# State-space mixer of a hybrid layer: decay exponents by two 32-row products, and the scaling of a chunk placed behind the next chunk's masked decays

## What is computed

```python
acum = cumsum(dt * a)                                     # per head, over the chunk's 64 tokens
seg = acum[..., :, None] - acum[..., None, :]
decay = where(causal, exp(where(causal, seg, 0)), 0)
y_diag = einsum(cb[:, :, None] * decay, xdt)              # cb = cm . bm, xdt = x * dt
y_off = einsum(cm, s_prev) * exp(acum)[..., None]
y = (y_diag + y_off + x * d_skip) * silu(z)
y = rms_norm(y per group) * norm_g
```

## Time and profile before

| what | value |
|---|---|
| median of 3 runs | 1448.69 us (1448.61 to 1450.59) |
| span of the profiled execution | 1447.4 us |
| the profiled execution's own time | not listed apart; the median is 1.3 us above its span |
| PE busy | 1422.7 us, 98% of the span |
| DVE, ACT, POOL busy | 727.2, 411.7, 221.4 us |
| state-space stage, PE | 465.07 to 621.40 us, five chunks of 31.27 us |

### The profile page before, as it was taken

The page is one execution under the profiler, slowest core; times in us unless marked ns, Lnnn a source line. Parts: engine busy times, 40 slices in busy tenths (PEclk is TensorE's granted clock), DMA queues, the critical chain, the costliest instruction groups (busy, mean ns, idle before and its releaser), DMA issues.

```text
span 1447.4 us, 32378 instructions
## 1 busy us (share of the span) xinstructions
PE 1422.7 (98%) x13553; PEld 1031.3 (71%) x13553; DVE 727.2 (50%) x1360; ACT 411.7 (28%) x847; POOL 221.4 (15%) x183
## 2 busy tenths in 40 slices
PE   7999999999999999999999999999999999999997
PEld 6999777677776777777779985864466766757752
DVE  7443778887755677735467654623312112211217
ACT  2333444443422454333533211111111111111112
POOL 3784113130110000020003000011010000000000
PEclk9999999999999999999999999999999999999999
DMA  7897573754244544566568639699999999999996
GB/s 286 190 194 155 129 219 105 205 174 134 73 132 141 140 119 120 185 184 190 150 228 209 213 115 388 244 402 413 425 427 428 428 427 428 428 428 425 430 410 264
DMA packets 157907, 375.76 MB, mean 260 GB/s; under 512 B 102241, under 2 KB 110833, under 8 KB 139841
## 3 DMA queue, kind: packets, MB, share of 16 engines
q1 hardware_dynamic: 141936, 346.64, 67.7%
q0 software_dynamic: 7152, 16.85, 3.4%
q10 hardware_dynamic: 8672, 10.20, 2.1%
HBM read 329.24 MB, written 51.95 MB: 263 GB/s over the span
## 4 chain that ended last, share of the span: by engine, by line
PE 88%; DVE 6%; DMA 2%; DVEq 2%; ACT 1%; issue 1%; SPq 0%; ACTq 0%
PE PS L725 22%; PE PS L1296 15%; PE PS L1315 8%; PE PS L742 7%; PE PS L1142 6%; PE PS L1263 6%; PE PS L809 3%; DVE region L1823 2%; PE PS L1184 2%; PE PS L1268 2%; DVE region L1830 2%; PE PS L1206 1%; DMA region<-w_in 1%; PE PS L817 1%; PE PS L1122 1%
## 5 line engine op out<-in xcount | busy, mean ns | idle before, releaser
L725 PE MATMUL PS<-h0T,region 128*128 128x320 f32 x1360 | 390.3, 438 | 2.9 <-issue 1.6
L1428 ACT ACTIVATE region<-PS 128x320 f32<-128x320 f32 (+5 forms) x351 | 146.0, 427 | 664.8 <-PE PS L725 227.8
L725 PEld LDWEIGHTS PS<-h0T,region 128*128 128x128 f32 x1360 | 251.6, 190 | 110.8 <-issue 12.9
L1296 PE MATMUL PS<-region 128*64 128x512 f32 x1024 | 228.1, 592 | 0.0
L1296 PEld LDWEIGHTS PS<-region 128*64 128x64 f32 x1024 | 117.6, 137 | 101.6 <-issue 49.8
L1823 DVE TENSOR_TENSOR region<-region 128x512 f32<-128x512 f32 (+10 forms) x237 | 165.4, 717 | 35.9 <-DMA region<-wo 5.7
L1428 ACT ACTIVATE region<-region 128x256 f32<-128x256 f32 (+10 forms) x229 | 99.5, 465 | 100.3 <-DVEq L2243 24.5
L1315 PE MATMUL PS<-region,history 128*64 128x512 f32 x512 | 119.2, 597 | 1.1 <-ACTq L1763 0.5
L1823 DVE TENSOR_TENSOR history<-region,PS 128x256 f32<-128x256 f32 x32 | 13.5, 421 | 200.5 <-ACTq L1758 200.5
L1428 ACT ACT_TABLE_LOAD x77 | 98.8, 1283 | 25.5 <-ACTq L1475 9.5
L1830 DVE SCALAR_TENSOR_TENSOR region<-region,feature_vectors 128x320 f32<-128x320 f32 (+1 forms) x103 | 76.9, 747 | 54.1 <-ACTq L1504 41.0
(11 more groups left out here) (248 smaller groups left out, 1582.8 us busy)
## 6 DMA issues: line engine op xcount, KB each, us to landing
region<-moe_w SPq DMA_DIRECT2D x65, 2048.0 KB, 29.8
region<-moe_w SPq DMA_DIRECT2D x65, 1024.0 KB, 28.5
region<-w_in SPq DMA_DIRECT2D x115, 512.0 KB, 5.6
region<-wo SPq DMA_DIRECT2D x32, 512.0 KB, 4.4
expert_rows<-region SPq DMA_DIRECT2D x20, 512.0 KB, 7.0
region<-expert_rows SPq DMA_DIRECT2D x5, 2048.0 KB, 16.6
projected<-region ACTq DMA_DIRECT2D x59, 167.5 KB, 3.6
region<-projected SPq DMA_DIRECT2D x10, 768.0 KB, 6.6
```

Source lines behind the costliest of these rows:

```text
L725: last = mm(PS[:, 6 + i % 2, 0:NTOK], WR[:, i, k, :], H0T[:, k, :], start=(k == 0), stop=(k == KT - 1))
L1296: last = mm(PS[tiles(i), 2, :], XE[:, k, tiles(i)], W13[r][i][:, k * 512:k * 512 + 512], start=(k == 0), stop=(k == KT - 1))
L1428: return nc.scalar.activation(out, in_, f, **kw)
```

## The change

The constants and vectors on rows 32 to 63 are copied to rows 64 to 95 as well: three small loads on SP, of the bias and `a` in VEC, of LH, and of the second half of PM (pairs 8 to 15) in the place of the first. PM and RD are 8 wide instead of 16: on rows 32 to 63 RD holds pairs 0 to 7, on rows 64 to 95 pairs 8 to 15. The dt rows of a chunk come by two transfers, rows 0 to 63 as before and rows 32 to 63 once more into 64 to 95 (for chunk 0 a third one for rows 96 to 127), and the waits for `rows_in` count by 32. Each product of L990 takes 32 rows instead of 128, the two on different rows. The rest of the chunk's program stays but for `late(c - 1)`, which DVE now does after the SEG products (`ss_mt`) instead of before `step_in(c + 1)`.

```diff
-        LH, PM, SEL, TRI = (CON[:, a:a + n] for a, n in ((C_LH, 128), (C_PM, 16), (C_SEL, 32), (C_TRI, 128)))
+        LH, PM, SEL, TRI = (CON[:, a:a + n] for a, n in ((C_LH, 128), (C_PM, 8), (C_SEL, 32), (C_TRI, 128)))
...
-        RD, SEG, EBC, YO, YC, SN = take(16, L), take(16, L), take(16, L), take(16, L), take(16, L), take(2048)
+        RD, SEG, EBC, YO, YC, SN = take(8, L), take(16, L), take(16, L), take(16, L), take(16, L), take(2048)
...
+            sp.wait_ge(sem("vectors_in"), 32)
+            sp.dma_start(VEC[64:96, V_DTB:V_ALOG + 1], io['vecs'][32:64, V_DTB:V_ALOG + 1]).then_inc(sem("vectors_in"), 16)
+            sp.wait_ge(sem("consts_in_or_rows_kept"), 16)
+            sp.dma_start(CON[64:96, C_LH:C_LH + 128], io['consts'][32:64, C_LH:C_LH + 128]).then_inc(sem("vectors_in"), 16)
+            sp.dma_start(CON[64:96, C_PM:C_PM + 8], io['consts'][32:64, C_PM + 8:C_PM + 16]).then_inc(sem("vectors_in"), 16)
             sp.wait_ge(sem("zeroed_or_fetch_index"), 1)
...
             def dt_rows(c):
                 sp.wait_ge(sem("rows_free"), c + 1)
-                sp.dma_start(UM, ut[T_MISC, :, c, HIST:CW]).then_inc(sem("rows_in"), 16)
+                sp.dma_start(UM[0:64], ut[T_MISC, 0:64, c, HIST:CW]).then_inc(sem("rows_in"), 16)
+                sp.dma_start(UM[64:96], ut[T_MISC, 32:64, c, HIST:CW]).then_inc(sem("rows_in"), 16)
+                if c == 0:
+                    sp.dma_start(UM[96:128], ut[T_MISC, 96:128, c, HIST:CW]).then_inc(sem("rows_in"), 16)
...
                 for k in range(2):
-                    last = mm(bank(3 + k, 8, L), LH, RD[:, 8 * k:8 * k + 8, :], **full)
+                    rows = slice(32 + 32 * k, 64 + 32 * k)
+                    last = mm(bank(3 + k, 8, L), LH[rows], RD[rows], **full)
...
             def step_in(c):
-                dve.wait_ge(sem("rows_in"), c * 16 + 16)
+                dve.wait_ge(sem("rows_in"), c * 32 + 48)
...
-                tt(RD, over(AC, 16, 0, L), PM.unsqueeze(2).to_broadcast([128, 16, L]), mul)
+                tt(RD, over(AC, 8, 0, L), PM.unsqueeze(2).to_broadcast([128, 8, L]), mul)
...
                 tt(XDT, banks(0, 2, 16, L), DTS.unsqueeze(2).to_broadcast([128, 16, L]), mul)
-                if c > 0:
-                    late(c - 1)
                 if c is not NPC:
                     step_in(c + 1)
...
                 dve.drain().then_inc(sem("ss_mt"), 1)
+                if c > 0:
+                    late(c - 1)
                 tt(XET, XDT, ALS.unsqueeze(2).to_broadcast([128, 16, L]), mul)
```

More of the change, by code:

```diff
@@ L355, in gla_in @@
         def gla_in(c):
-            return ("conv_in" if c % 2 else "rows_in"), 16 * NCH + 32 * (c // 2 + 1)
+            return ("conv_in", 16 * NCH + 32 * (c // 2 + 1)) if c % 2 else ("rows_in", 32 * NCH + 16 + 32 * (c // 2 + 1))
         def rows_in_at(c):
@@ L1038, in _ @@
             pe.wait_ge(sem("phase_over"), ENG * 2)
+            pe.wait_ge(sem("vectors_in"), 80)
             for c in range(NCH):
@@ L1599, in _ @@
             meet(act, 2)
+            act.wait_ge(sem("vectors_in"), 80)
             a_(NA, VEC[:, V_ALOG:V_ALOG + 1], ACT.Exp)
@@ L2243, in ssm @@
                 dve.drain().then_inc(sem("variance"), 1)
+            dve.wait_ge(sem("vectors_in"), 80)
             step_in(0)
```

## The result

The changed kernel takes 1453.65 us (median of 11 runs, 1451.26 to 1456.59), the kernel before 1449.89 in the same comparison (11 runs, 1448.61 to 1452.49). The ratio is 1.0026, with a 95% interval of 1.0018 to 1.0034: 3.8 us slower, where 3.9 was forecast. The profiled execution itself took 1455.11 us at a span of 1453.2.

A forecast was written before the change was run, and what follows sets the result against it. PE bounds the kernel now, with the ring 0.43 us behind; moving late() makes the ring bound chunks 1 to 3. Waits 5.18 less 1.25 gained give +3.9 on 1448.69: 1452.6 us, range 1449.4 to 1455.4 for 8 in 10.

The forecast's parts named there:

- The ring: State-space mixer: DVE, ACT, SP's row loads, DVE again, one turn per chunk; 0.43 us from bounding, then 33.79, 32.59, 33.29.
- The sum: Five chunks: PE waits of 5.18 less 5 x 0.25 gained, +3.9 us on 1448.69, giving 1452.6 us; chance 0.60.
- PE would stay the bound: Rival: chunk 1's dt rows land within 5.98 us with nothing added, only the product's gain is left, 1447.4 us; chance 0.14.
- the second transfer lands 1.6 us behind the first: Rival, dt rows: the second transfer adds 1.6 us instead of 0.3 in three turns, 1456.5 us; chance 0.08.
- the pair runs one behind the other: Rival, two products of L990: they keep 1.80 us, plus 0.20 behind them, giving 1453.5 us; chance 0.08.
- the staircase: L990: second product starts with the first's second pass; 1.35 us instead of 1.80, less 0.20 behind, 0.25 net per chunk.
- The rival on full overlap: L990: both products run fully beside each other, 0.90 us instead of 1.35, giving 1451.7 us; chance 0.10.
- The waits before L1026: PE in chunks 1 to 3 waits for ss_yr from DVE: 1.32, 1.58 and 2.28 us.
- a wait for ss_mt instead of ss_yr: Sign of being wrong: PE waits before L1018, so ss_mt is late; the SEG products were forecast in time, at 511.6.
- The clock: PE in the five chunks: times were taken at a granted clock of 1.00, one chunk being 31.27 us.
- The second transfer: Dt rows of each chunk: their second part, issued behind the first on SP, adds 0.3 us per turn, between 0 and 0.6.
- The small loads at the RWKV stage: Three loads of VEC and CON on SP cost nothing: 1.95 us of cover for three issues of about 0.4.

The follow-up runs named there:

- The second trace: The changed kernel run once more, unedited, to see whether the clock drop in chunk 2 comes again: 1453.21 us, one run.

## Why the prediction was right, step by step

**The ring: right, shown.** The single terms measured what was put in. Root to conv issue: 504.66 - 499.67 = 4.99 (4.99 put in). Step_in to YO: 520.11 - 511.45 = 8.66 (8.60). YO to the next root: 532.59 - 520.11 = 12.48 (12.48). The turns, from reciprocal to reciprocal (497.85, 530.78, 564.79, 597.37), are 32.93, 34.01 and 32.58, 99.52 in all; the prediction had 33.79, 32.59 and 33.29, 99.67 in all. Each was off by about as much as its landing: from the first issue of the dt rows to step_in it took 6.37, 7.26 and 6.01 us where 7.3, 6.1 and 6.8 had been put in. From the first product of chunk 0 to that of chunk 4 took 128.81 us against 125.07 before, +3.74; the prediction had +4.15.

**The sum: near, in part by luck.** The single chunks were not met: 31.50, 35.45 and 31.15 us where 32.3, 32.6 and 33.3 had been forecast. Their sum is 98.10 against 98.2, since what the long landing and the drop of the clock added to chunk 2 came off chunk 3, and the misses of the landings largely cancelled. In the five chunks PE waited 4.40 us where 5.18 was forecast, and its own work fell by 0.67 (156.33 to 155.66) where 1.25 was forecast: the pair gave 2.75 in five chunks, the drop of the clock took 1.71 of it back, and 0.37 went into the first products behind the waits. That is +3.73 against +3.93. Without the drop PE's work would have been less and its waits longer, so the two misses are not independent; the mechanism stands on the experiments, not on this agreement.

**The rivals.** That PE would stay the bound needed 5.98 us or less in chunk 1; it was 6.37, a near miss. That the second transfer lands 1.6 us behind the first is not borne out: 0.5, 1.4 and 0.3. That the pair runs one behind the other is excluded by its 1.06 us.

**The pair: the gain was there, the staircase was not.** The step said "a staircase: the second product starts with the first's second pass", 1.35 us and 0.20 behind. The pair took 1.06 and the projection the 0.20 more: 0.55 net per chunk instead of 0.25. The start times show two records at 500.33 and two at 500.86, so both first passes run together, and then both second passes. Of the 1.06, 0.86 is two passes of 0.43, and 0.2 stands in front of them. Its cause is not shown, but the records fit a weight load that is less covered: the pair's first begins 0.07 us before the product ahead ends, where on 128 rows it begins 0.19 before. Of the 0.2, 0.1 is there on 128 rows as well (1.80 is four passes of 0.43 and 0.08; on one group of 32 rows it is 1.91). L1026's 1.93 reads the same way: the time of eight full-array records, 1.74, plus 0.2; I had taken the 0.2 for a staircase. The rival on full overlap was true in its mechanism, at 1.06 instead of its 0.90, and the Trainium skill (TensorE: Matmul & The Clock Gate, Part 3) had it right: matmuls in different row groups ran together; the trace agrees, 1.06 against 1.91 on one group. As the prediction said, this gain counts only where PE is the bound, so the total came out some 0.6 us lower than forecast by chunks 0 and 4, and by the turns of the ring not at all.

**The waits before L1026: right in kind.** Forecast 1.32, 1.58 and 2.28 us; measured 0.71, 2.00 and 0.35. In chunk 2 PE waited before L1027 too, 0.95, so ss_mt was late as well, after the longest way from issue to step_in, 7.26. The prediction had named a wait for ss_mt instead of ss_yr as a sign of being wrong; in this one chunk it came beside the wait for ss_yr.

**The clock: missed.** The prediction put a granted clock of 1.00 everywhere. The drop cost PE 1.71 us in chunk 2, but most of it was hidden: YO to root took 12.69 there (553.92 to 566.61) instead of 12.48, since DVE, not PE, set the turn. As an estimate, the 1.5 us that the ring did not lose came off PE's wait in chunk 3, which was 0.35 instead of the forecast 2.28.

**The carried state: missed.** PE waited 0.4 us in chunk 4. Its load follows the store of the old state, 7.55 us, and takes 6.30 more.

**The second transfer: sized at 0.3, none seen** when one transfer took the place of two. **The small loads at the RWKV stage: nothing shown.** The kernels with them start the state-space stage at 466.38 to 468.68, those without at 464.73 to 467.77, which overlap. In the first trace after, SP issues them from 143.12 to 144.51. PE is 1.15 us behind the trace of before once it has 200 records, 44.7 us into the span, and 1.14 behind once it has 1500, at 184.3, so no cost is seen there. In the profiled execution the stage began 3.7 us later than before; 1.15 of it came in the first 35 us, ahead of every edit, and the rest in small steps in the RWKV stage. The second trace began at 466.81. I take that as spread between executions; no run shows its cause. The 3.8 us of the medians are what the stage gives, from its first product to the next stage's first: 156.66 before, 160.32 and 160.59 in the two traces after.

## What to carry to other kernels

When PE is busy all the time, look for the ring of waits just behind it and read its slack, here 0.43 us: work moved out of the time that covers a transfer then costs its length less that slack in every turn, though no engine has more to do. Here 2.80 less 0.43 was to be expected, and with late() alone moved the three chunks grew by 1.25, 2.89 and 1.79 us, 1.98 in the mean. And look at the order in which a queue issues its loads: a small load that needs nothing should not stand behind one that waits for another engine; that alone turned a loss of 0.26% into a gain of 0.14%. A gain on PE inside such a ring should show only in the turns that PE still bounds; that is argued from the sums, and no run changes the pair alone.

## What the runs showed of the hardware that was not expected

- Two fp32 products of 512 columns on different groups of 32 rows take 1.06 us together, 1.80 on all rows one behind the other, 1.91 on one group of 32. Of the 1.06 some 0.2 is more than the two passes of 0.43, 0.1 of it more than the pair on all rows pays, and the full-array projection behind takes another 0.2 (4.50 instead of 4.31).
- The granted clock fell to half for 3.4 us behind a PE wait of 2.0 us, at the same place in both traces of the changed kernel, but not behind the same waits (0.8, then 2.0) in another kernel and not behind 2.5 us in a third. Twice in one trace (mean 0.75 over 6.2 us in chunk 2) it fell with no wait ahead of it, right behind two products on one group of 32 rows.
- A transfer of 32 KB and the same as two of 16 and 8 KB land equally late behind one of 768 KB: 6.0 to 7.0 against 6.0 to 7.3 us.
